# Four weight slots, and three product tiles side by side at each norm of a two-block transformer kernel

## The reference

```python
def rmsnorm(x, g):                       # eps 1e-6; divides by the root of the mean square of a position
    return x * rsqrt(mean(x * x, -1) + eps) * g

def first_block(x, ...):
    h_res = concatenate([meta, x])                       # 528 x 1024
    proj = rmsnorm(h_res, g_mix_pre) @ w_in              # u_a, c_g, b_g, v_b, gate logits
    y_a = real(fft2(u_a)) @ w_fourier                    # over positions and 128-wide channel groups
    y_b = (b_g * conv3(c_g * v_b)) @ w_conv_out
    merged = sigmoid(gate_a) * y_a + sigmoid(gate_b) * y_b
    h_res = h_res + rmsnorm(merged @ w_out, g_mix_post)
    a, v = split(conv3(rmsnorm(h_res, g_ffn_pre) @ w_up))   # 1024 -> 2 x 2816
    return h_res + rmsnorm((gelu(a) * v) @ w_down, g_ffn_post)

def second_block(x, ...):
    q, k, v, glu_in, gates = split(rms_norm(x, norm_mix_pre) @ w_in)
    y_a = dilated_attention(q, k, v) @ w_attn_out        # 12 heads in 3 groups of dilation 1, 4, 16
    c = silu(layer_norm(conv31(c_val * sigmoid(c_gate)))) # glu_in = c_val, c_gate
    mixed = sigmoid(g_a) * y_a + sigmoid(g_c) * (c @ conv_pw)
    x = x + rms_norm(mixed @ w_out, norm_mix_post)
    a, v = split(causal_conv3(rms_norm(x, norm_ffn_pre) @ w_up))
    return x + rms_norm((gelu(a) * v) @ w_down, norm_ffn_post)
```

## Time and profile before

| | us |
|---|---|
| median of 3 runs | 1700.87 (1700.36 to 1701.6) |
| the profiled execution | 1702.98 |
| its span, first to last instruction | 1701.2 |
| PE busy | 1630.9 (96%) |
| VectorE busy | 1136.2 (67%) |
| ScalarE busy | 558.4 (33%) |
| GpSimd busy | 69.1 (4%) |

### The profile page before, as it was taken

How to read it: one execution, slowest core, us unless ns; L and a number is a source line. 1 busy time by engine, 2 the same in 40 slices (tenths; PEclk the granted TensorE clock), 3 DMA queues, 4 the chain that set the end, 5 groups by cost and what they waited for, 6 DMA issues and landing times.

```text
span 1701.2 us, 25558 instructions
## 1 busy us (share of the span) xinstructions
PE 1630.9 (96%) x9386; PEld 1432.2 (84%) x9386; DVE 1136.2 (67%) x1551; ACT 558.4 (33%) x719; POOL 69.1 (4%) x69
## 2 busy tenths in 40 slices
PE   7999999799999999979999999999997999999995
PEld 6999999799999988758887888887885788888884
DVE  5334555578888842278899888875455888888324
ACT  4222323432222232243333334467334322222221
POOL 3010000110000000020000000000001100000001
PEclk9999999889999999979999999999998999999998
DMA  4352212212222222312322222212222222222232
GB/s 152 108 164 99 86 50 92 69 63 86 99 86 87 98 99 101 109 50 95 105 87 75 90 90 75 90 62 89 85 99 74 74 96 90 97 99 99 101 109 74
DMA packets 44845, 155.41 MB, mean 91 GB/s; under 512 B 5338, under 2 KB 5850, under 8 KB 44800
## 3 DMA queue, kind: packets, MB, share of 16 engines
q1 hardware_dynamic: 41760, 147.26, 24.9%
q0 software_dynamic: 1312, 4.91, 1.0%
q10 hardware_dynamic: 1728, 2.62, 0.5%
HBM read 152.65 MB, written 6.06 MB: 93 GB/s over the span
## 4 chain that ended last, share of the span: by engine, by line
PE 88%; DVE 9%; ACT 2%; issue 1%; DMA 0%; DVEq 0%; SPq 0%; ACTq 0%
PE ps L400 82%; DVE work L1291 3%; PE ps L627 1%; PE ps L608 1%; DVE res L1036 1%; DVE wlo L979 1%; DVE xl L1007 1%; PE ps L486 1%; DVE tmp L1031 1%; PE ps L615 1%; ACT whi L671 1%; PE ps L570 1%; DVE x2l L1007 0%; PE ps L540 0%; DMA raw<-w_dram 0%
## 5 line engine op out<-in xcount | busy, mean ns | idle before, releaser
L400 PE MATMUL ps<-xh,whi 128*128 128x258 f32 (+2 forms) x2048 | 584.6, 334 | 27.9 <-DVE xl L1007 16.4
L400 PE MATMUL ps<-xh,wlo 128*128 128x258 f32 (+2 forms) x2048 | 574.6, 329 | 0.0
L400 PE MATMUL ps<-xl,whi 128*128 128x258 f32 (+2 forms) x2048 | 574.2, 329 | 0.0
L671 ACT ACTIVATE whi<-raw 128x1024 fp32r<-128x1024 f32 x272 | 287.9, 1059 | 654.3 <-PE ps L400 653.4
L979 DVE TENSOR_TENSOR wlo<-raw,whi 128x1024 fp32r<-128x1024 f32 x270 | 330.1, 1223 | 223.9 <-ACT whi L671 223.2
L400 PEld LDWEIGHTS ps<-xh,whi 128*128 128x128 f32 x2048 | 349.8, 192 | 69.3 <-issue 22.4
L400 PEld LDWEIGHTS ps<-xh,wlo 128*128 128x128 f32 x2048 | 349.1, 191 | 33.5
L400 PEld LDWEIGHTS ps<-xl,whi 128*128 128x128 f32 x2048 | 350.4, 192 | 32.0 <-issue 1.0
L1291 DVE SCALAR_TENSOR_TENSOR work<-cin,vecs,work 128x512 f32<-128x512 f32 x240 | 180.1, 750 | 6.8
L400 PE MATMUL ps<-fl,whi 128*128 128x512 f32 x352 | 136.9, 389 | 0.0
L400 PE MATMUL ps<-fh,wlo 128*128 128x512 f32 x352 | 136.9, 389 | 0.0
(11 more groups left out here) (180 smaller groups left out, 1597.7 us busy)
## 6 DMA issues: line engine op xcount, KB each, us to landing
raw<-w_dram SPq DMA_DIRECT2D x272, 512.0 KB, 3.2
bias_copies_dram<-bias_rows_dram POOLq DMA_DIRECT2D x12, 320.0 KB, 4.1
res<-x_dram SPq DMA_DIRECT2D x8, 264.0 KB, 7.0
bias<-bias_copies_dram ACTq DMA_DIRECT2D x8, 256.0 KB, 2.9
out_dram<-res SPq DMA_DIRECT2D x8, 256.0 KB, 2.0
dftp<-dftp_dram POOLq DMA_DIRECT2D x1, 550.7 KB, 5.2
bias<-bias_copies_dram ACTq DMA_DIRECT2D x4, 128.0 KB, 2.0
vecs<-vec_dram SPq DMA_DIRECT2D x1, 364.0 KB, 7.7
```

The costliest lines, as they stand in the source:

```text
L400: last = pe.matmul(ps[:, 2 * pair + h, 0:b - a], w[:, slot, cols], xx[:, k, a:b], start=start and n == 0, stop=stop and n == 2)
L671: act.activation(whi[:, slot, :], raw[:, slot, :], ACT.Copy).then_inc(w_hi, 1)
```

## The change

**Slots.** `raw` and `whi` get four slots; `wlo` has no memory of its own but lies in `raw`'s, and the low part is written over the piece. SP therefore loads piece n+4 when PE has used piece n, and the split of piece n+3 stands in the programs of ScalarE and VectorE where that of n+2 stood.

**Norms.** `norm_tiles` takes the place of `first_two_tiles`. At up1, glu and up2 three tiles advance together: for each k a step of tile 0, of tile 1 and of tile 2. At u they lie two steps apart. Then comes tile 3 alone, with `sum_channels` in its middle and `spread_inverse` behind it. More PSUM banks are used at once (`PAIRS_OF`), and in u and up1 ScalarE copies the first tiles out unscaled (`unscaled`, `BY_ACT`).

**Squares.** ScalarE makes the high parts of all eight k first, and the squares behind them. VectorE adds them into `acc` (`inverse_of_res`), behind the low parts; GpSimd does no such work. Between the squares stand the splits of pieces 4 and 5.

**Taps.** The taps begin at the fifth of the eight turns in glu (20 there, 35 before), and the first 23 slots of heads take 6 taps each (the first 9 before).

**Down.** PE waits for all tiles of an up product to be read before the down product; the down products use four PSUM banks in turn.

The diff, cut to its core:

```diff
-TAPS_TO = [(KD - 1) * sum(TAPS_A_GLU)]
+TAPS_FROM = 4
+TAPS_TO = [(KD - TAPS_FROM) * sum(TAPS_A_GLU)]
 for _s in range(SLOTS):
-    TAPS_TO.append(min(TAPS_TO[-1] + (6 if _s < 9 else 5), TAPS * KD))
+    TAPS_TO.append(min(TAPS_TO[-1] + (6 if _s < 23 else 5), TAPS * KD))
...
+PAIRS_OF = {"u": (0, 3, 1, 0), "up1": (0, 3, 1, 0, 3, 1, 0, 2, 3, 1, 0, 1),
+            "glu": (0, 1, 2, 3, 5, 6, 7, 3), "up2": (0, 1, 2, 3, 5, 6, 7, 3)}
+BY_ACT = {"u": 3, "up1": 4, "glu": 0, "up2": 0}
...
-        raw = put("raw", [P, 2, PIECE])
-        whi = put("whi", [P, 2, PIECE], F32R)
-        wlo = put("wlo", [P, 2, PIECE], F32R)
+        raw_at = at[0]
+        raw = put("raw", [P, SLOTS_W, PIECE])
+        wlo = put("wlo", [P, SLOTS_W, PIECE], F32R, offset=raw_at)
+        whi = put("whi", [P, SLOTS_W, PIECE], F32R)
...
-                    sp.wait_ge(w_split, it * 2 + (s - 1))
+                    sp.wait_ge(w_used, it * SLOTS_W + (s - SLOTS_W + 1))
...
+            def norm_tiles(phase, operand, spans, ready, norm, lags=(0, 0, 0)):
+                pairs = PAIRS_OF[phase]
+                for step in range(KD + lags[-1]):
+                    for p, lag in enumerate(lags):
+                        k = step - lag
+                        if not 0 <= k < KD:
+                            continue
+                        if k == 0:
+                            pe.wait_ge(w_split, C0[phase] + p + 1)
+                            if T0[phase]:
+                                pe.wait_ge(tile_read, T0[phase])
+                        if p == 0:
+                            pe.wait_ge(operand_ready, ready + k + 1)
+                        last = three_passes(pairs[p], p, k, k, operand, spans, k == 0, k == KD - 1)
                         if k == KD - 1:
                             last.then_inc(w_used, 1)
+                for n in range(len(lags), len(pairs)):
+                    before = [m for m in range(n) if pairs[m] == pairs[n]]
+                    one_piece_tile(phase, n, n % 4, pairs[n], before[-1] + 1 if before else 0, operand, spans,
+                                   (lambda: sum_channels(norm)) if n == 3 else None)
+                    if n == 3:
                         spread_inverse(norm)
...
+                norm_tiles(up, operand, spans, READY[h_name] - KD, norm)
+                tiles_after_norm(up, 2 * KFF, operand, spans)
+                pe.wait_ge(tile_read, T0[dn])
...
+            norm_tiles("u", (xh, xl), all1, 0, "pre1", (0, 2, 4))
...
                     act.activation(dst(k), res[:, k, a:b], ACT.Identity, scale=vec(gain, k)).then_inc(x_hi, 1)
-                    if landed is not None and k < 2:
-                        w_to_hi(0, k)
+                    if landed is not None and k % 2 == 0:
+                        w_to_hi(phase, 0, k // 2)
+                for k in range(KD):
                     if k >= 2:
-                        act.wait_ge(sqp_used, SQP[name] + k - 1)
+                        act.wait_ge(sqp_used, SQP[name] + max(k - 1, 2))
                     act.activation(sq[:, k % 2, 0:b - a], res[:, k, a:b], ACT.Square).then_inc(sqp_ready, 1)
+                    if k == 1:
+                        for n in range(min(BY_ACT[phase], 3)):
+                            unscaled(phase, n, b - a)
+                    if k in (4, 6):
+                        w_to_hi(phase, 0, 2 + k // 2)
                 act.preload_act_table(ACT.Sqrt)
-                piece_used(phase, 0)
-                w_to_hi(C0[phase] // 2 + 1, 0)
                 root(name)
...
+            def inverse_of_res(phase, name, width):
+                for k in range(1, KD):
+                    dve.wait_ge(sqp_ready, SQP[name] + k + 1)
+                    if k == 1:
+                        dve.tensor_tensor(acc[:, 0:width], sq[:, 0, 0:width], sq[:, 1, 0:width], ALU.add) \
+                           .then_inc(sqp_used, 2)
+                    else:
+                        dve.wait_ge(sqp_used, SQP[name] + k)
+                        dve.tensor_tensor(acc[:, 0:width], acc[:, 0:width], sq[:, k % 2, 0:width], ALU.add) \
+                           .then_inc(sqp_used, 1)
+                    if k in (4, 6):
+                        w_to_lo(phase, 0, 2 + k // 2)
+                inverse(name)
...
+                def two_pairs(it):
+                    it_n = 4 * it if isinstance(it, int) else len(PAIRS_OF[up])
+                    for h in range(2):
+                        for s in range(2):
+                            n = 2 * h + s
...
+                            if n == 3 or it_n:
+                                w_to_lo(up, it, n + 3)
```

More of the change, by code:

```diff
@@ L228, in two_block_kernel @@
         dft_landed = sem("dft_landed")
-        w_landed = [sem("w_landed0"), sem("w_landed1")]
+        w_landed = [sem(f"w_landed{s}") for s in range(SLOTS_W)]
         w_hi = sem("w_hi")
@@ L290, in tile_psum, with stat @@
         def tile_psum(pair, two):
-            return ps[:, 2 * pair:2 * pair + 2, 0:H1] if two else ps[:, 2 * pair, :]
+            return ps[:, 2 * pair:2 * pair + 2, 0:H1] if two else ps[:, pair, :]
+        def stat(name):
+            w, blocks = NORMS[name]
+            return ps[:, STAT, :] if blocks == QB else ps[:, STAT:STAT + 2, 0:w * blocks // 2]
         def groups_of(i):
@@ L381, in _ @@
             pool.wait_ge(bias_spread, 16 * NG * HEADS)
-            add_squares_of_res("pre1f", N1)
-            add_squares_of_res("pre2", SEQ)
-            add_squares_of_res("pre2f", SEQ)
             pool.wait_ge(rstd_ready, 6)
@@ L432, in first_two_tiles @@
                         if k == KD - 1:
                             last.then_inc(w_used, 1)
-                    if k >= lag:
-                        last = three_passes(1, 1, k - lag, k - lag, operand, spans, k == lag, k == KD + lag - 1)
-                    if norm is not None and k == KD + 0:
-                        sum_channels(norm, accp)
-                    if norm is not None and k == KD + 1:
+                for n in range(len(lags), len(pairs)):
[3 more added lines that the diff above has]
+                    if n == 3:
@@ L439, in first_two_tiles @@
                         spread_inverse(norm)
-                last.then_inc(w_used, 1)
+                    if n == 6 and phase == "up1":
+                        pe.wait_ge(rstd_ready, NTH[norm] // 2)
             def start_tiles(phase, operand, spans, ready, ahead):
@@ L635, in mid_tile @@
                 if n == MEAN_AT + 3:
-                    sum_channels("ln", acc)
+                    sum_channels("ln")
                 if n == MEAN_AT + 4:
@@ L726, in up_body @@
                 def up_body(it, first=False):
-                    for s in range(first, 2):
-                        piece_used(up, it * 2 + s)
-                        w_to_hi(it + (C0[up] // 2 + 1), s)
-                    act.wait_ge(a_ready, it + (1 + KFF * (up == "up2")))
-                    act.activation(work[:, 1, 0:SEQ], work[:, 0, 0:SEQ], ACT.Gelu_apprx_tanh).then_inc(gelu_ready, 1)
+                    for s in range(4):
+                        if s == 3 or not first:
+                            w_to_hi(up, it, s + 3)
+                        if s % 2:
+                            act.wait_ge(a_ready, it * 2 + (s // 2 + 1 + KFF * (up == "up2")))
+                            act.activation(work[:, 1, 0:SEQ], work[:, 0, 0:SEQ], ACT.Gelu_apprx_tanh) \
+                               .then_inc(gelu_ready, 1)
                 up_body(0, True)
-                with act.Fori(1, KFF) as it:
+                with act.Fori(1, KFF // 2) as it:
                     up_body(it)
@@ L1094, in ffn @@
                 dve.wait_ge(rstd_ready, 2 if up == "up1" else 5)
-                pair(0, True)
-                loop(KFF, 7, pair, 1)
+                first = len(PAIRS_OF[up]) // 4
+                for it in range(first):
+                    two_pairs(it)
+                loop(KFF // 2, 14, two_pairs, first)
                 start_sum(SEQ)
                 def down_body(it, more=True):
-                    for m in range(2):
+                    for m in range(4):
                         for c in range(3):
-                            n = it * 6 + (3 * m + c)
@@ L1271, in _ @@
                         lambda k: cut_lo("pre2", k, "norm_mix_pre_2", N_META, L1, lambda k: x2h[:, k, :],
-                                         lambda k: x2l[:, k, :]))
-            step(dve.memset(stage[:, :, 0:2], 0.0))
+                                         lambda k: x2l[:, k, :]), "glu")
+            inverse_of_res("glu", "pre2", SEQ)
             step(dve.memset(cin2[:, :, 0:TAPS - 1], 0.0))
-            inverse("pre2")
-            w_to_lo("glu", 0, 0)
             dve.wait_ge(rstd_ready, 3)
@@ L1325, in _ @@
             for it in range(KD):
-                glu(it, it == 0)
+                glu(it)
             def biased_scores(n):
```

555 lines of the change are left out of this document (268 added, 287 removed).

## The result

| | before | after |
|---|---|---|
| median, us (six runs each) | 1700.84 | 1709.11 |
| ratio, 95% interval | | 1.0046 (1.0036 to 1.0056) |
| span of the profiled execution, us | 1701.2 | 1707.6 |
| PE busy, us | 1630.9 | 1625.0 |
| VectorE / ScalarE / GpSimd busy, us | 1136.2 / 558.4 / 69.1 | 1127.9 / 566.3 / 20.0 |

The changed kernel is slower by 8.3 us; 1703.6 was forecast, 1693 to 1709 as the range, so the result stands at the range's upper end. The two profiled executions differ by 6.4. The other 1.9 is that the profiled execution of before lay 2.1 over its median, which the prediction says, and that of after only 0.2 over its own.

What follows compares the result with a forecast made beforehand. PE, busy for 1630.9 of 1701.2 us, bounds the kernel, and the norms decide. Terms 2.0 - 3.4 - 2.0 - 2.0 + 1.9 + 2.9 + 1.9 + 2.1 - 0.7 = +2.7 on 1700.9 gave 1703.6 us, range 1693 to 1709.

Steps and rivals of the forecast that it cites:

- The sum of squares is late: In tile 3 at four norms, PE waits for VectorE's last addition: 4.9 us at pre2 and pre2f, 5.4 at u and pre1f.
- The two chains: To the late sum: piece 4's transfer at pre2 and pre2f (9.0 us); ScalarE's copies of tiles at u and pre1f (8.3).
- The low clock behind it: After the sums' wait, clock low for another 4.4 us: 4 steps of tile 3 take 4.8 us in place of 2.7.
- The ramp: Three tiles advancing at the norms: PE has 24 steps, sets the pace, no gaps; 4.3 us of low clock from the start.
- VectorE begins late: At up1 and up2, PE waits for tile 6's split (+1.7 and +2.4 us) and tile 7 (+0.2 and +0.5).
- Down: At both entries to down, PE waits for the last up tile to be read: 0.95 us each, +1.9 in all.
- Heads: 15 taps moved from glu to slots 9 to 22 of heads fill VectorE: +2.1 us, bounds 0.7 and 6.5.
- none beyond 25: A sign in heads: longer waits for probabilities in slots 10 to 17, and none in slots beyond 25.
- rival 3: Heads turn to VectorE's pace, each attention block handing on its lag: 6.5 us in place of 2.1, 1708; chance 0.17.
- Splits: More slots relieve PE's waits for the split of a piece: 0.7 of 1.7 us, at out1, so -0.7.
- Rival 1: Ramps go at VectorE's pace: 2.4 us less at pre2, 7.2 at three norms, 1696.4; chance 0.25 together with rival 2.
- Rival 2: The clock holds at the waits and the taps are absorbed: -7.1 us, 1693.8; chance 0.25 together with rival 1.

Runs made afterwards that it cites:

- e2: Changed kernel with only the splits of pieces 4 and 5 moved behind the squares; 1687.58 us, 0.9922 of the kernel before.
- e1: Changed kernel with all eight squares and their additions ahead of ScalarE's copies of the first tiles and the splits of pieces 4 and 5; 1678.33 us, ratio 0.9869.
- e8: e1 with the split of piece 6 of up1 and up2 right behind the inverse root, and piece 7's where piece 6's stood; 1679.12 us, 0.9866.
- e10: e9 with e7's earlier entry into down, and the splits of pieces 6 and 7 behind VectorE's read of the first and third tile; 1672.14 us, 0.9821.
- e6: e1 with the old table of taps (35 in glu, six a slot for the first nine slots); 1679.77 us, 0.9876.
- e4: Changed kernel with squares beside the high parts, added by GpSimd, and the splits of pieces 4 and 5 behind; 1689.90 us, 0.9935.
- e12: e10 with unread matmuls filling PE's idle time at the program's start and around the sums and spread ahead of three ramps; 1668.87 us, 0.9815.
- e5: Changed kernel with twenty unread matmuls of 512 columns filling PE's wait ahead of the sums; 1698.06 us, 0.9986.
- e9: e1 with the inverse root ahead of the roundings and splits of pieces 4 and 5; 1677.34 us, 0.9857.
- e7: e1 with PE entering each down product once the banks of its first tiles are read, not all; 1677.71 us, 0.9856.
- e13: e12 without the 36 matmuls at the start; 1666.65 us, 0.9793.

## Why the prediction was right, and where it was off

- **The sum of squares is late: right.** Forecast 4.9 us (pre2, pre2f) and 5.4 (u, pre1f), measured 5.1, 5.3, 5.1 and 5.1. The two chains were the right ones (e2). It decided the sign: with those sums on time the same slots and the same three tiles gain 22.5 us (e1).
- **The low clock behind it: the mechanism right, one size too small.** No trace of before has such a wait ahead of sums, and the 4.4 us of low clock behind it were my estimate. In the changed kernel the granted clock was 0.50 from 757.4 to 764.2, 1337.7 to 1344.4, 358.1 to 364.8 and 33.8 to 44.0 (pre2, pre2f, pre1f, u), and the second half of tile 3 took, in this order, 4.8, 4.4, 4.3 and 5.4 us against 4.8 forecast. But the term "end of the sums (0.9)" was taken at the upper level; the sums stand inside the low stretch and took 1.7 to 1.8. That is +0.8 at each norm, and the earlier trace rows have the doubled 0.43 beside 0.227.
- **The ramp: bound by PE, as forecast, without gaps.** My terms come from the passes of the earlier trace rows: 0.227 us for 512 columns and 0.240 for 516, both at a granted clock of 1.00. That makes 0.68 and 0.72 a step, 2.04 and 2.17 a k of three steps. At 0.50 a pass is 0.43, a step 1.3 and a k 3.9, so that PE's k is longer than VectorE's 1.99 at either level. The 0.735 a step of u was an estimate; the changed kernel has 0.73 there (passes 0.244 apart from 13.30 to 25.98). "I take 4.3 of low clock from the start" was short at two places: it lasted 5.7 us at pre2, 5.3 at pre1f, 4.4 at pre2f. From first pass to wait the three took, in this order, 22.1, 22.8 and 21.5 us against 21.1, 22.1 and 21.1. Together with the sums, the norms gave back 4.2 us and not 7.4; this is most of what the forecast lacks. In u the sums (+0.9) and the second half (+0.6) were offset by a start 1.1 us ahead of the 9.4 forecast and a wait 0.3 shorter.
- **VectorE begins late: right.** +1.9 and +2.8 in up1 and up2, against 1.9 and 2.9. The splits' order decides a part of it: e8 and e10 took the waits at tile 6 away, 3.5 us, and 1.0 and 1.9 us of them came back at later tiles.
- **Down:** 1.5 and 1.2 instead of 0.95 each. PE idles for 1.33 and 1.17 us there.
- **Heads: the size right (+2.3 against +2.1), the reason only half.** I put it down to 15 taps moved out of glu. e6 moved them back and gained nothing: VectorE, which starts glu with four tiles to read where it had two, has no room for them there. By this the lag from the norm is the cost, and the taps only decide where it is paid; no run has the new table of taps with the old norm. The waits fell at the first, third and fifteenth of 16 blocks; "none beyond 25" was wrong, the last is at 1125.36 (0.41 us). In nine slots VectorE was busy for 64.0 of 66.4 us, against the earlier trace rows. The chain of work that ended last, followed back from release to release, says the same: from 880 to 1140 us it lies on PE's passes for 23.5% and on VectorE's taps for 30.0%, where before it was 65.3% and 6.3%. So VectorE does set the pace in heads, as rival 3 says, but at the price of the sum.
- **Splits: the 0.7 was right.** The table has -1.7 at out1 and its norm, but only the 0.74 that PE waited there before (at 286.23) is a split's. Another 0.7 is the way from the spread of post1 to the first pass of up1, 6.39 us before and 5.69 here. It is 6.40 in e1 and 5.44 in e4, so it moves by as much without this change.
- **Rival 1** was wrong for this kernel. But its 2.4 us per norm is what came out, 2.5 at pre2, once e12 kept the clock up (2.6 at pre2f, 0.8 at pre1f). **Rival 2** was half tested by e5: where the clock held, 2.4 to 3.2 us per norm came back, not 2.1 (4.8 less 2.7; four times that is the 8.4 of its sum). **Rival 3** gave a total near the measured one, but not by its term: heads was at 2.3, not 6.5.
- The measured 8.3 lies 1.9 above the profiles' 6.4, as told above. The interval of the ratio, 6.1 to 9.5 us, holds both 8.3 and 6.4, but not the forecast 2.7. The measured time also lies outside the 1700 to 1707.5 that I gave my sum. That the wide range reaches just to 1709 is partly luck: about 3.7 us are terms that were too small, and 1.9 are the distance of two profiled executions from their medians.
- **Two slips in the working.** The terms of u give 45.0 - 43.21 = 1.8, not 2.0. And rival 2 has rows 5 against it, whose low passes at 357.92 are no fall by idle time: PE was busy for 14.33 of the 15.30 us from 340.0 to 355.3. The rows that do bear on such a fall are those of e5 and e12.

What stays open: why the same piece 5 at pre2 lands 4.2 us after it is asked for in e1 and 6.7 in e8, and how much of e9's and e7's small gains is real.

## What to carry to other kernels

When a reduction is taken off a slow engine, its place in the other engines' programs can decide more than its cost (30.8 us here, e1): put what a stalled TensorE waits for ahead of everything that itself waits for a transfer or for TensorE. Price an idle TensorE at its wait plus the low clock behind it, some 2 to 3 us in this kernel, whether the wait was 5 us (e5) or 3 (e2), and count the short instructions directly behind it at the low clock too: eight sums took 1.73 us here and not 0.8. Four tiles in place of two multiplied ahead of each norm left VectorE, which reads them, behind by as much. This showed up later as waits (1.5 and 2.0 us at tile 6 of the ups), of which a local reordering took back about half (e10).

## What the runs showed of the hardware

- The low clock at the start of a ramp could be bought off. With the idle time ahead of it filled, the granted clock at pre2 was 1.00 from the first pass on (e12, 714.6 to 733.7) and the passes followed at 0.23 us from the second on; in e10 it was 0.50 up to 718.1, with passes 0.43 us apart. The mean granted clock of the execution rose from 0.983 (e10) to 0.994 (e13), while the time fell by 5.5 us.
- The fill at the start of the program brought the passes behind it no closer together. The 36 matmuls of 128 columns of e12 came back to back for 7.7 us at 0.21 us each. That is the spacing of the eight spreads, also of 128 columns, where the granted clock was 0.50: they took 1.97 us there and 1.01 at 1.00 (both in the changed kernel, the first below, the second at 764.75 above), 0.21 and 0.11 from one start to the next. Behind the 36, passes of two matmuls of 264 columns followed at 0.44 us for another 4.9 us (11.55 to 16.4) and at 0.24 from there on; in e13 they followed at 0.44 for 4.6 us from 7.99, with no fill ahead. For all of this start the traces give a granted clock of 1.00, so only the spacing tells of it, and no run shows what made it wide.
- By the rows of the spreads a matmul of 128 columns is no quarter of one of 512: 0.11 us against 0.227 at a granted clock of 1.00, 0.21 against 0.427 at 0.50.

```profile
1306.96 1.97 PE L500 MATMUL ps<-ident_r,inv 128*128 128x128 f32 x8 [1.40 <-DVE inv L1019]
```

- Idle time of like length did not always bring the clock down: 1.26 us ahead of the sums of pre1f did in e5 (granted clock 0.50 from 358.3 to 361.7), 1.34 us ahead of tile 3 at the same norm in e12 did not (1.00 from 345.2 to 352.0), and nor did 1.96 us ahead of tile 6 of up2 in e9 (1.00 from 1320 to 1345).
- Sums of one column and spreads did not bring the clock down where no wait stood ahead of them (e9, at all four norms: 1.00 from 28 to 50, 345 to 365, 725 to 745 and 1300 to 1330). The low passes at 357.92 in the earlier trace rows, in a stretch with a granted clock of 0.50 from 355.3 to 358.7, come behind such a spread too; none of the runs isolates their cause.
- A low part of VectorE beside an addition of GpSimd took 1.78 us and not 0.74 (e4 at pre2: 722.90, 728.28 and 733.65 beside one, 726.29 and 731.67 beside none).
